# Expert stages of an encoder block: long and short products in turn, against two long and then two short

## The reference, cut to what matters

```
s   = scores of 8 heads x 2 halves x 128 keys; the 16 best pairs of keys per head and token
idx = first key * 128 + second key            # one of 16384 experts
g   = softmax of the 16 picked scores
a   = gelu(x @ expert_u[idx])                 # one number per token and picked expert
y   = sum over picks of g * a * expert_v[idx]
```

## Time and profile before

| what | value |
|---|---|
| median of three runs | 931.26 us |
| the profiled execution's own time | 932.53 us |
| its span, first to last instruction | 930.7 us |
| mean granted TensorE clock | 0.997 |
| wide u tiles (long and short matmuls) | 366.6 to 589.0 us |
| v stage | 594.4 to 921.0 us |
| long matmuls, u stage and v stage | 672 and 1021 |
| weight loads, mean recorded duration | 187 to 191 ns |

### The profile page before, as it was taken

The page is one execution under the profiler, slowest core; times in us unless marked ns, Lnnn a source line. Parts: engine busy times, 40 slices in busy tenths (PEclk is TensorE's granted clock), DMA queues, the critical chain, the costliest instruction groups (busy, mean ns, idle before and its releaser), DMA issues.

```text
span 930.7 us, 20171 instructions
## 1 busy us (share of the span) xinstructions
PE 916.7 (98%) x6644; PEld 880.5 (95%) x6644; DVE 805.8 (87%) x1654; ACT 572.7 (62%) x1060; POOL 396.0 (43%) x234
## 2 busy tenths in 40 slices
PE   9999999999999899999999999999999999999997
PEld 9999989999999899999999999989999989999997
DVE  7988877887799898898999876779999899999986
ACT  6555774656645365888778766555555455555555
POOL 0000000047697786578878868223133323233400
PEclk9999999999999999999999999999999999999999
DMA  8877658666487698899989999999999999999991
GB/s 299 266 235 227 198 177 254 191 224 220 156 247 223 194 243 220 239 296 256 261 253 251 264 265 254 293 391 395 401 383 359 403 399 385 399 347 395 391 327 46
DMA packets 137736, 261.33 MB, mean 281 GB/s; under 512 B 31200, under 2 KB 80480, under 8 KB 137408
## 3 DMA queue, kind: packets, MB, share of 16 engines
q1 hardware_dynamic: 110688, 225.72, 72.5%
q0 software_dynamic: 26544, 33.89, 13.4%
q10 hardware_dynamic: 432, 0.80, 0.3%
HBM read 234.94 MB, written 25.36 MB: 280 GB/s over the span
## 4 chain that ended last, share of the span: by engine, by line
PE 78%; DVE 10%; DMA 4%; ACT 4%; issue 3%; SPq 1%; ACTq 0%; DVEq 0%
PE pOO L1531 29%; PE pOO L1539 5%; PE pMM L1539 5%; PE pTT L1842 5%; PE pOO L1842 5%; PE pMM L1842 5%; PE pSS L1842 5%; DMA raw<-in_vrows 4%; PE pOO L1540 3%; PE pMM L1540 3%; PE pTT L1843 2%; PE pMM L1843 2%; PE pOO L1843 2%; PE pSS L1843 2%; DVE wlos L981 2%
## 5 line engine op out<-in xcount | busy, mean ns | idle before, releaser
L700 ACT ACTIVATE whis<-raw 128x1024 fp32r<-128x1024 f32 x326 | 343.3, 1055 | 145.0 <-PE pSS L1843 87.3
L675 POOL DMA_INDIRECT g_scratch<-small x117 | 209.3, 1789 | 49.6 <-issue 33.5
L1531 PE MATMUL pOO<-xpair,whis 128*128 128x224 f32 (+1 forms) x1184 | 209.0, 280 | 3.1 <-issue 3.1
L1531 PEld LDWEIGHTS pOO<-xpair,whis 128*128 128x128 f32 x1184 | 181.9, 192 | 5.5 <-issue 5.3
L1418 DVE TENSOR_TENSOR wlos<-raw,whis 128x1024 fp32r<-128x1024 f32 x125 | 152.7, 1221 | 26.5 <-ACT whis L700 23.8
L1531 PE MATMUL pOO<-xpair,wlos 128*128 128x224 f32 (+1 forms) x592 | 164.6, 278 | 0.0
L640 POOL TENSOR_TENSOR wlos<-raw,whis 128x1024 fp32r<-128x1024 f32 x30 | 72.1, 2412 | 215.2 <-ACT whis L700 215.1
L981 DVE TENSOR_TENSOR wlos<-raw,whis 128x1024 fp32r<-128x1024 f32 x118 | 143.3, 1218 | 10.9 <-ACT whis L700 5.3
L1531 PEld LDWEIGHTS pOO<-xpair,wlos 128*128 128x128 f32 x592 | 113.4, 192 | 0.0
L1539 PE MATMUL pMM<-xpair,whis 128*128 128x448 f32 x336 | 107.8, 372 | 0.0
L1539 PE MATMUL pOO<-xpair,whis 128*128 128x448 f32 x336 | 107.4, 373 | 0.1
(11 more groups left out here) (303 smaller groups left out, 2193.2 us busy)
## 6 DMA issues: line engine op xcount, KB each, us to landing
raw<-in_stream SPq DMA_DIRECT2D x199, 512.0 KB
raw<-in_vrows SPq DMA_DIRECT2D x128, 512.0 KB
a_scratch<-ast SPq DMA_DIRECT2D x128, 112.0 KB
held<-a_scratch SPq DMA_DIRECT2D x128, 112.0 KB
g_scratch<-ghot SPq DMA_DIRECT2D x32, 256.0 KB, 4.5
G<-g_scratch SPq DMA_DIRECT2D x124, 64.0 KB
biasm<-in_bias SPq DMA_DIRECT2D x8, 256.0 KB, 5.7
g_scratch<-small POOLq DMA_INDIRECT x128
```

The source lines that it names most:

```text
L675: pool.indirect_dma_start(g_dram, bass.IndirectOffsetOnAxis(goff[:, n:n + 1], 0), gval[:, h, k:k + 1], None, compute_op=ALU.add).then_inc( ...
L700: act.activation(whi[s], raw[s][:], ACT.Copy).then_inc(hi_ready, 1)
L1531: last = pe.matmul(dst, st, mv, start=(opening and c == 0 and q == 0), stop=(closing and c == len(terms) - 1 and q == 2))
```

## The change

Chunks are taken in pairs. For chunks c and c + 1 the kernel before issues long(c), short(c), long(c+1), short(c+1). The changed kernel issues long(c), long(c+1), short(c), short(c+1), in `halves_product` and in `v_tile`. Operands, target banks, columns, the first and last marks of the accumulation, waits and the semaphore on a tile's last matmul are as they were. A part of a tile in a G step has four chunks, and so two whole pairs. Tile 0 and the last three tiles of the v stage are left in the old order.

```diff
@@ halves_product
-                for c, (sh, sl, mv) in enumerate(terms):
+                def wide_one(c):
+                    sh, _, mv = terms[c]
                     pe.matmul(both, sh, mv, start=opening and c == 0, stop=False)
-                    last = pe.matmul(bank[:, 0:NU], sl, mv[:, 0, :], start=False, stop=closing and c == len(terms) - 1)
+                def narrow_one(c):
+                    _, sl, mv = terms[c]
+                    return pe.matmul(bank[:, 0:NU], sl, mv[:, 0, :], start=False, stop=closing and c == len(terms) - 1)
+                for c in range(0, len(terms), 2):
+                    wide_one(c)
+                    wide_one(c + 1)
+                    narrow_one(c)
+                    last = narrow_one(c + 1)
@@ v_tile
-                for c in range(C):
-                    last = v_products(i, s, c, c == C - 1 and isinstance(i, int) and i == NE_TILES - BY_BLOCK - 1)
+                closing = isinstance(i, int) and i == NE_TILES - BY_BLOCK - 1
+                for c in range(0, C, 2):
+                    v_wide(s, c)
+                    v_wide(s, c + 1)
+                    v_narrow(s, c)
+                    last = v_narrow(s, c + 1, c + 1 == C - 1 and closing)
                 last.then_inc(tile_done, 1)
```

More of the change, by code:

```diff
@@ L1836, in _, with v_wide, v_narrow @@
             pe.wait_ge(gbanks_free, 2 + G_STEPS)
+            def v_wide(s, c, opening=False):
+                pe.matmul(wide[c], whi[s][:, c, :], gpair[s], start=opening, stop=False)
+            def v_narrow(s, c, closing=False):
+                return pe.matmul(acc[c][:, 0:NU], wlo[s][:, c, :], ghi[s], start=False, stop=closing)
             def v_products(i, s, c, closing=False, dst=None, opening=False):
@@ L1841, in v_products @@
                 if dst is None:
-                    pe.matmul(wide[c], whi[s][:, c, :], gpair[s], start=opening, stop=False)
-                    return pe.matmul(acc[c][:, 0:NU], wlo[s][:, c, :], ghi[s], start=False, stop=closing)
+                    v_wide(s, c, opening)
+                    return v_narrow(s, c, closing)
                 for n, (st, mv) in enumerate(((whi, ghi), (whi, glo), (wlo, ghi))):
@@ L1855, in v_tile @@
                 v_wait(i)
-                last = None
-                for c in range(C):
-                    last = v_products(i, s, c, c == C - 1 and isinstance(i, int) and i == NE_TILES - BY_BLOCK - 1)
+                closing = isinstance(i, int) and i == NE_TILES - BY_BLOCK - 1
[4 more added lines that the diff above has]
+                    last = v_narrow(s, c + 1, c + 1 == C - 1 and closing)
                 last.then_inc(tile_done, 1)
```

## The result

| | before | changed |
|---|---|---|
| median of 20 runs each | 932.16 us | 934.94 us |
| lowest and highest | 926.45, 938.55 | 930.31, 942.00 |
| ratio, 95% interval | | 1.0042 (1.0024 to 1.0060) |
| profiled execution, its span | 932.53, 930.7 us | 931.65, 929.8 us |
| wide u tiles, first to last long | 222.1 us | 223.9 us |

The changed kernel is slower by 0.42%, about 3.9 us (2.2 to 5.6); the medians alone differ by 2.8 us. The forecast was no change. The range of 926 to 938 us holds the result, but the likeliest case (929 to 934 us) did not come about. That the range holds it is owed to its reach towards rival 2, and not to the argument for zero.

A forecast was written before the change was run, and what follows sets the result against it. TensorE was taken to bound the wide u tiles and v stage. A group cost 626.7 ns before and 201.6 + 201.6 + 111.7 + 111.7 = 626.6 after, so the 931.26 us median plus 0 gave 931.3 us, range 926 to 938.

The forecast's parts named there:

- the likeliest case: Whole kernel: no change, 929 to 934 us, chance 0.62.
- rival 2: Groups of both stages: every long costs 213 ns whatever precedes it, 11 ns more a group, 940.5 us; chance 0.22.
- the argument for zero: Groups of four matmuls: two of four loads stand under a short in both orders, so 0 ns a group.
- rival 1: Groups of both stages: loads run two ahead under two longs, up to 17 ns less a group, 917 us; chance 0.16.
- Bank, tile boundary and `tile_done`: Both stages: changed target-bank order costed at nothing; a tile's last short ends where it did, so `tile_done` keeps its time.
- What a long costs undisturbed: Long matmuls in both stages: the pair's 313.3 ns less 111.7 for the short leaves 201.6 ns.
- the short's turn: Short matmul in a pair: costs 111.7 ns, as in runs of 32-column and of 224-column matmuls.
- The 0.20 us behind the G step: Long behind a 256-column matmul whose streaming covers its load: recorded 0.20 us, taken as a test of the long's 201.6 ns.

The follow-up runs named there:

- e5: Changed kernel with short matmuls cut to 128 columns and the v stage back in the old order: v tile 2.507 us, wide u tile 2.534 us.
- e6: Changed kernel, v tiles 1 to 124 issuing one matmul per chunk, 448 falling to 224 columns: gaps 190 ns at 416 columns, 119 at 256.
- e7: Changed kernel with one matmul in four left out: long, long, short takes 520 ns (v stage); long, short, short 426.5 ns (u stage).
- e4: Changed kernel without the short matmuls of v tiles 1 to 124: longs a median 207 ns apart, v stage 319.8 us.
- e2: Changed kernel with groups of four longs and four shorts in both stages: v tile 2.534 us, ratio 1.0035 (1.0006 to 1.0063).
- e3: Kernel before, old order, with the long matmul's data in one contiguous run of 448 numbers: ratio 0.9997 (0.9972 to 1.0021).

## Why the prediction was wrong in its likeliest case

**What held.** TensorE bounds both stages, at full clock, and waits stayed small (2.5 us in the v stage, 0.5 in the u stage). One load runs ahead and never two (the loads of after, e5), so rival 1 had no ground. Under a short only the load counts (e5), under a long the stream: the gap falls with the columns (e6). Bank, tile boundary and `tile_done` cost nothing: a v tile takes four times its group, and the groups of both stages are alike although one stays in a bank and the other changes it. The records came out much as foreseen: the second long's gap is 0.20 to 0.21 us, its median duration 368 ns in the v stage and 366 in the u stage, against 373 or 374 for the first.

**The step that failed** is a term of the sum: "What a long costs undisturbed is 313.3 - 111.7 = 201.6 ns, if the short's turn costs the 111.7 of rows 8 and 9." The if was wrong. Rows 8 and 9 are runs in which every matmul waits for its load. In the old order a short stands alone between two longs, and its turn is cheaper. With the long at 206.7 ns (e7; 205 to 207 in e4) the lone short is left with 313.3 - 206.7 = 106.6 ns. A short behind a short costs 113.2 (e7), near the 111.7 of the runs.

With these prices a group in the new order costs 2 x 206.7 + 106.6 + 113.2 = 633.2 ns; the trace has 633.3. That is 6.6 ns more for each of 832 groups, 5.5 us, where the prediction had 0. For e2's group of eight, 4 x 206.7 + 106.6 + 3 x 113.2 = 1273 against 1267 measured. The old order would take 1253, so the prices foresee 20 ns more and the trace has 14: they hold for pairs and are too high for runs of four.

Which matmul of the group pays is less sure. The starts of the loads, which e5 shows to be what stays apart, lie 108.3 ns apart across a short and 205.1 across a long in the old order (means of some 1000 each, v stage). In the new order they lie 108.4 ns apart across the first short and 110.8 across the second, then 209.1 across the long behind them and 205.0 across the other long. So some 2.5 of the 6.6 ns lie at the load that follows another without a long between, and some 4 at the long behind the two shorts. That a load on an idle load path costs less than one behind another load fits the first part. The second part no run explains.

Why loads in a row stand further apart than a lone one was not tested either. The size is suggestive. The Trainium skill (TensorE: Matmul & The Clock Gate, LDWEIGHTS) gives a load in ns as its columns / 1.2, by which 128 columns come to an estimate of 106.7 ns. The lone short's 106.6 agrees with that, the 111.7 to 113.2 of shorts in a row do not.

**How the error could have been seen.** The 0.20 us behind the G step was read as 201.6, which the other term asked for, while the finer starts say 202 to 204 for 46 of the 47 such longs, in the median 203. With 203 the group comes to 2 x 203 + 2 x 111.7 = 629.4 ns, 2.3 us in all: two fifths of the 5.5. A test that is rounded to 10 ns cannot confirm a sum that turns on 2 ns a group.

**Rival 2** had the sign right and its mechanism half. Long behind two shorts is indeed 213. But the other long did drop to 205 where it had 213, so its 638 ns and 940.5 us were too much. It had 0.22, and its lower edge of 934 us is about where the result lies.

**What stays open.** The sum of 5.5 us against 3.9 (2.2 to 5.6) measured. They agree within the interval; whether part of the loss falls into waits that were there anyway, the timed runs are too scattered to say (in the profiled v stage TensorE waited 0.7 us less). Why the long behind two shorts costs more, and why loads in a row do, is open. None of the kernels beats the one before.

## What to carry to other kernels

Where long and short matmuls are mixed and each has a weight load of its own, count the loads that stand under a short matmul, and keep these apart: in turn (long, short) was the best of the three orders here, and two shorts in a row cost 6.6 ns more, four in a row some 14. Regrouping hid no load here, since only one ran ahead, however much room the longs had. And do not take the price of a lone operation from a run of the same operations when the sum is multiplied by hundreds: read it as the difference of two patterns, from starts many repetitions apart.

## What the runs showed that I had not expected

- With all short matmuls gone from 124 v tiles, the v stage is only 6.8 us shorter (e4: 319.8 against 326.6 us). VectorE's data are nearly as late as TensorE (70.1 us of waits for them), with VectorE busy for 296.18 us and a DMA share of 1.00, so work on TensorE alone can win little more than that there.
- Contiguous data made the long matmuls of the u stage dearer, 316.6 ns a pair against 313.3, and left those of the v stage alone (e3).
- A matmul's excess over its columns tends to grow with the width, from 12 ns at 256 columns to some 18 to 20 at 448 (e6, e4).
- With shorts of 128 columns a long starts 0.06 us behind the start of its own load, where it was 0.10 before, and it is the next load that comes later (e5).
